# One-hot tiles of the expert gates: four single-token comparisons on VectorE replaced by one wide comparison there and a multiplication on GpSimd

## The chip, the cores and the metric

The kernel runs on one core of a Trainium2 chip. The metric is the device time of one execution in microseconds (us). Engines are named TensorE (PE in the profile), VectorE (DVE), ScalarE (ACT) and GpSimd (POOL). All data is 32-bit floating point.

## The reference

The reference is a chain of two small networks on 256 tokens with 1024 features. The last stage of each of the second network's two layers is a mixture over 16384 single-neuron experts. For each token, 8 heads choose 16 experts each, so 128 slots per token. An expert's number is a pair (i1, i2) of numbers below 128, and each slot has a weight `gate`:

```python
expert = i1 * PEER_NKEYS + i2
gate = jax.nn.softmax(score, axis=-1)
h = jnp.einsum('thkd,td->thk', u_tab[expert], zb)
act = gate * jax.nn.gelu(h, approximate=False)
return jnp.einsum('thk,thkd->td', act, v_tab[expert])
```

The kernel doesn't gather experts. It computes all 16384 for all tokens and multiplies by a dense table of gates, G[t, i1, i2], which is the sum of the weights of the token's slots that chose (i1, i2). For one token this table is a product of two matrices with the 128 slots as the summed dimension: A[slot, i1] = gate x (i1 is the slot's first number), B[slot, i2] = (i2 is the slot's second number). Both are one-hot in each row. The stage `PeerGates` builds A and B and multiplies them.

## The kernel before

The program is a list of stages. Each has a part for each engine, and the engines meet between stages at one counter, `stage_done`. Weights stream all the time through a ring of four blocks. Each block is split for the products into a rounded part (ScalarE, `round`) and the rest (GpSimd, `leave_rest`, L253, a tensor_tensor of 128x1024 that subtracts the one from the other). In the stage `Modulation`, at the program's start, VectorE takes over half of these subtractions, so that both engines run L253.

In a layer, `PeerRoute` finds the chosen experts with VectorE and GpSimd. Two of its lines return below. L2297 is a VectorE comparison (is_equal) of 128x512 elements, of a rank broadcast along the last dimension against the first 16 columns of the table of numbers. L2236 is GpSimd's multiplication of the resulting 128x256 elements in place by a broadcast row. L2241 adds halves on GpSimd. `PeerRoute` ends with a transpose that leaves `slot`, of shape [128 slots, 3, 256 tokens]: first number, second number, weight.

`PeerGates` then goes through the tokens in 128 sets of two (`SET = 2`), with four buffers (`BUFS = 4`) for the one-hot tiles `hot` of shape [128, buffer, A or B, token, 128]. For each token VectorE compares the constant row `iota` (0 to 127) with the token's column of `slot`: at L2356 against the first number, multiplying by the weight in the same instruction, and at L2357 against the second number. TensorE waits for `hot_ready` and issues one matmul per token (L2370) into PSUM; each appears as two records in the profile. ScalarE copies the 128x256 results of a set into the table of gates (L2386). VectorE waits for TensorE's `done` of the set that used its buffer before; TensorE waits for ScalarE's `kept`. GpSimd has no part in this stage. VectorE's part is written out without a loop; TensorE and ScalarE loop.

The stage `PeerExperts` follows, with products of 128x256 (L237 to L239) and the two VectorE instructions L2522 and L2525 per block. Its first instruction on VectorE is a memset, at L2515, which waits for the end of the gate stage.

Of the kernel before, what the change touches and what calls it, by code (L numbers as in the profile page):

```python
# [2 lines left out]

# [8 lines left out]
ALU = mybir.AluOpType  # L12
AX = mybir.AxisListType

P = 128
# [57 lines left out]
class Signals:  # L73


    def __init__(self, nc, ctx):
        self.nc, self.ctx, self.sems, self.total = nc, ctx, {}, {}
# [94 lines left out]
class Stage:  # L172
# [83 lines left out]
    def pe(self, pe):  # L256
        pass
# [4 lines left out]
    def dve(self, dve, link):  # L262
        pass

    def pool(self, pool, link):
        rounds = self.split // RING
        if rounds > 1:
            with pool.Fori(0, rounds) as it:
                for r in range(RING):
                    for h in range(2):  # L270
                        self.leave_rest(r, h, self.split_count(it * RING + r))
        else:
            rounds = 0
        for j in range(rounds * RING, self.split):
            for h in range(2):
                self.leave_rest(j, h, self.split_count(j))
# [49 lines left out]
class Modulation(Stage):  # L326
# [68 lines left out]
    def dve(self, dve, link):  # L395
        c, nc = self.chip, self.nc
        dve.wait_ge(self.chip.stage_done, self.index)
        dve.wait_ge(self.cond_rounded.sem, self.cond_rounded.at(1))
        nc.vector.tensor_tensor(self.parts[:, :, 2:4], self.cond, self.parts[:, :, 0:2].bitcast(F32), ALU.subtract)\
            .then_inc(self.cond_split.sem, 1)  # L400
        with dve.Fori(0, self.blocks // RING) as it:
            for r in range(RING):
                self.leave_rest(r, 1, self.split_count(it * RING + r), nc.vector)
        dve.wait_ge(self.turned.sem, self.turned.at(1))
        m = c.mods[:].rearrange("p j d s -> p (j d) s")
        b = columns(c.vec, "b_mod", self.layer, 72).unsqueeze(2).broadcast_to([P, 72, 2])
        turned = c.ps[:, 7, 0:288].rearrange("p (m s) -> p m s", s=4)
        link(nc.vector.tensor_tensor(m, turned[:, :, 0:2], b, ALU.add))
        link(nc.vector.tensor_tensor(m, m, turned[:, :, 2:4], ALU.add))
        for n in range(3):  # L410
            g = columns(c.vec, "norm_g", 3 * self.layer + n, KD).unsqueeze(2).broadcast_to([P, KD, 2])
            scale, gate = c.mods[:, 3 * n + 1, :, :], c.mods[:, 3 * n + 2, :, :]
            link(nc.vector.tensor_scalar(scale, scale, 1.0, None, ALU.add))
            link(nc.vector.tensor_tensor(scale, scale, g, ALU.mult))
            if n != 1:
                link(nc.vector.tensor_scalar(gate, gate, 0.5, None, ALU.mult))
        if self.start:
            dve.wait_ge(c.inputs_loaded, 16 * N_INPUTS)
            dve.wait_ge(self.start.stored.sem, self.start.stored.at(16))
        dve.sem_inc(c.stage_done, 1)  # L420


class Norm(Stage):
# [48 lines left out]
    def pe(self, pe):  # L472
# [6 lines left out]
        if self.keep:  # L479
# [3 lines left out]
            last.then_inc(self.x_kept.sem, 1)  # L483

    def dve(self, dve, link):
        c, nc = self.chip, self.nc
        dve.wait_ge(self.chip.stage_done, self.index)
# [1840 lines left out]
class PeerGates(Stage):  # L2328
# [9 lines left out]
    def __init__(self, chip):  # L2338
        super().__init__(chip)
        self.slot = chip.at(G_SLOT, 3, N)  # L2340
        self.hot = chip.at(G_HOT, self.BUFS, 2, self.SET, P)
        self.gates = chip.at(G_GATES, N * NKEYS)
        self.hot_ready = chip.signals("hot_ready", self.SETS)
        self.done = chip.signals("gates_done", self.SETS)
        self.kept = chip.signals("gates_kept", self.SETS)

    def dve(self, dve, link):
        v, iota = self.nc.vector, self.chip.iota
        dve.wait_ge(self.chip.stage_done, self.index)
        for n in range(self.SETS):  # L2350
            r = n % self.BUFS
            if n >= self.BUFS:
                dve.wait_ge(self.done.sem, self.done.at(n - self.BUFS + 1))
            for i in range(self.SET):
                first, second, gate = [self.slot[:, a, n * self.SET + i:n * self.SET + i + 1] for a in range(3)]
                v.tensor_scalar(self.hot[:, r, 0, i], iota, first, gate, ALU.is_equal, ALU.mult)  # L2356
                last = v.tensor_scalar(self.hot[:, r, 1, i], iota, second, None, ALU.is_equal)  # L2357
            last.then_inc(self.hot_ready.sem, 1)

    def pe(self, pe):  # L2360
        pe.wait_ge(self.chip.stage_done, self.index)

        def body(it, first=False):
            for r in range(self.BUFS):
                n = it * self.BUFS + r
                pe.wait_ge(self.hot_ready.sem, self.hot_ready.at(n + 1))
                if not first:
                    pe.wait_ge(self.kept.sem, self.kept.at(n - self.BUFS + 1))
                for i in range(self.SET):
                    last = self.nc.tensor.matmul(self.chip.ps[:, r, i * P:(i + 1) * P], self.hot[:, r, 0, i], self.hot[:, r, 1, i],  # L2370
                                                 start=True, stop=True)
                last.then_inc(self.done.sem, 1)

        body(0, first=True)
        with pe.Fori(1, self.SETS // self.BUFS) as it:
            body(it)
# [481 lines left out]
```

## Time and profile before

| | |
|---|---|
| median of three runs | 5390.88 us (5387.66 to 5395.12) |
| profiled execution, its own time | 5387.66 us |
| its span, first to last instruction | 5385.6 us |
| busy: TensorE, GpSimd, VectorE, ScalarE | 4776, 2937, 2793, 1934 us |
| the two gate stages | 117.3 and 117.4 us |

Busy shares are averages over stages with different limits. A group's busy time counts each instant once, and its mean is that of one instruction from start to end; where instructions of an engine overlap, the mean is longer than the distance from start to start.

### The profile page before, as it was taken

The numbers are of one execution on the slowest core, as the hardware profiler recorded it, in microseconds if no ns is written. First come the engines' busy times: TensorE is split into PE (matmuls) and PEld (weight loads), VectorE is DVE, ScalarE is ACT, GpSimd is POOL, SyncE is SP. The second block draws the span as 40 slices with busy tenths as digits, with TensorE's granted clock in tenths as the row PEclk, the third lists the DMA queues.
The fourth block names the chain that finished last, engine by engine and source line by source line (L and its number), as shares of the span: only waits on it lengthen the run. The fifth ranks groups of instructions, "written<-read, shape, count | busy, mean of one in ns | idle before, by whom it ended". The sixth has DMA issues, their size and how long they took to land.

```text
span 5385.6 us, 77857 instructions
## 1 busy us (share of the span) xinstructions
PE 4776.2 (89%) x30280; PEld 4183.4 (78%) x30280; DVE 2793.4 (52%) x4012; ACT 1934.3 (36%) x2791; POOL 2937.4 (55%) x1298
## 2 busy tenths in 40 slices
PE   6899899969999989898874899999898865999998
PEld 2587777727778879787873899999877864899998
DVE  6410221182110431345569777777444669777776
ACT  5322332262223234332232444444431233444443
POOL 6444144484434358651262588887640351688886
PEclk9999999999999999987787999999986888999999
DMA  8322122272223234440030344445430120344443
GB/s 311 117 94 89 53 78 94 100 267 86 94 79 109 86 118 173 151 164 1 24 126 0 114 174 177 173 176 181 154 133 1 48 102 0 134 178 172 178 173 139
DMA packets 92447, 649.46 MB, mean 121 GB/s; under 512 B 9824, under 2 KB 14048, under 8 KB 14432
## 3 DMA queue, kind: packets, MB, share of 16 engines
q1 hardware_dynamic: 87120, 634.25, 32.9%
q10 hardware_dynamic: 5136, 12.49, 0.6%
q8 instruction: 141, 2.31, 0.2%
q14 instruction: 50, 0.41, 0.0%
HBM read 642.50 MB, written 4.19 MB: 120 GB/s over the span
## 4 chain that ended last, share of the span: by engine, by line
PE 59%; DVE 21%; DMA 8%; issue 5%; POOL 4%; ACT 3%; ACTq 0%; SPq 0%; POOLq 0%; DVEq 0%
PE ps L237 16%; PE ps L238 16%; PE ps L239 16%; DMA ring<-in_weights 8%; DVE part L2525 5%; POOL ring_rest L253 4%; DVE arena L2356 2%; DVE arena L2357 2%; PE ps L1334 1%; PE ps L477 1%; DVE arena L506 1%; PE ps L1302 1%; ACT part L2477 1%; DVE arena L1963 1%; ACT rounded L224 1%
## 5 line engine op out<-in xcount | busy, mean ns | idle before, releaser
L253 POOL TENSOR_TENSOR ring_rest<-ring,rounded 128x1024 fp32r<-128x1024 f32 x1104 | 2776.0, 2537 | 1893.1 <-ACT rounded L224 1365.7
L237 PE MATMUL ps<-part,rounded 128*128 128x256 f32 (+1 forms) x5760 | 1853.4, 322 | 151.5 <-DVE part L499 64.7
L238 PE MATMUL ps<-part,rounded 128*128 128x256 f32 (+1 forms) x5760 | 1835.5, 319 | 0.0
L239 PE MATMUL ps<-part,ring_rest 128*128 128x256 f32 (+1 forms) x5760 | 1827.0, 317 | 0.0
L237 PEld LDWEIGHTS ps<-part,rounded 128*128 128x128 f32 x5760 | 1101.5, 191 | 285.9 <-issue 67.7
L238 PEld LDWEIGHTS ps<-part,rounded 128*128 128x128 f32 x5760 | 1101.2, 191 | 77.4
L239 PEld LDWEIGHTS ps<-part,ring_rest 128*128 128x128 f32 x5760 | 1095.1, 190 | 70.9
L224 ACT ACTIVATE rounded<-ring 128x1024 fp32r<-128x1024 f32 x672 | 671.1, 1050 | 800.6 <-PE ps L239 713.2
L2525 DVE TENSOR_TENSOR part<-arena,part 128x256 fp32r<-128x256 f32 x256 | 605.7, 2366 | 211.3 <-ACT part L2477 211.3
L2492 ACT ACTIVATE rounded<-ring 128x1024 fp32r<-128x1024 f32 x504 | 531.7, 1055 | 410.0 <-DMA ring<-in_weights 408.1
L237 PE MATMUL ps<-x_parts,rounded 128*128 128x256 f32 x2304 | 652.3, 283 | 12.2 <-DVE x_parts L499 11.0
L238 PE MATMUL ps<-x_parts,rounded 128*128 128x256 f32 x2304 | 653.8, 284 | 0.0
L239 PE MATMUL ps<-x_parts,ring_rest 128*128 128x256 f32 x2304 | 649.5, 282 | 0.0
L2522 DVE TENSOR_TENSOR arena<-arena 128x256 f32<-128x256 f32 x256 | 530.4, 2072 | 183.9 <-ACT arena L2471 183.6
L237 PEld LDWEIGHTS ps<-x_parts,rounded 128*128 128x128 f32 x2304 | 439.9, 191 | 14.3 <-issue 12.6
L238 PEld LDWEIGHTS ps<-x_parts,rounded 128*128 128x128 f32 x2304 | 437.8, 190 | 0.0
L239 PEld LDWEIGHTS ps<-x_parts,ring_rest 128*128 128x128 f32 x2304 | 434.5, 189 | 0.0
L586 DVE TENSOR_TENSOR part<-ps,arena 128x512 f32<-128x512 f32 (+1 forms) x88 | 55.0, 625 | 525.2 <-ACT arena L575 525.2
L648 DVE SCALAR_TENSOR_TENSOR x<-ps,mods,x 128x256 f32<-128x256 f32 x80 | 31.9, 475 | 522.1 <-PE ps L239 522.1
L575 ACT ACTIVATE arena<-ps 128x512 f32<-128x512 f32 (+1 forms) x88 | 47.9, 544 | 572.8 <-PE ps L239 572.7
L2471 ACT ACTIVATE arena<-ps 128x256 f32<-128x256 f32 x256 | 98.5, 385 | 406.6 <-PE ps L239 377.8
L253 DVE TENSOR_TENSOR ring_rest<-ring,rounded 128x1024 fp32r<-128x1024 f32 x72 | 228.0, 3193 | 6.7 <-ACT rounded L224 6.7
(324 smaller groups left out, 4805.4 us busy)
## 6 DMA issues: line engine op xcount, KB each, us to landing
ring<-in_weights SPq DMA_DIRECT2D x600, 1024.0 KB, 4.8
arena<-bias_scratch ACTq DMA_DIRECT2D x2, 2048.0 KB, 8.7
bias_scratch<-arena ACTq DMA_DIRECT2D x1, 3072.0 KB, 8.7
x<-in_x SPq DMA_DIRECT2D x1, 2048.0 KB, 20.7
arena<-in_keys ACTq DMA_DIRECT2D x2, 1024.0 KB, 4.9
arena<-in_bias_in SPq DMA_DIRECT2D x1, 1216.0 KB, 8.5
arena<-in_cst SPq DMA_DIRECT2D x1, 1216.0 KB, 21.8
arena<-in_expo ACTq DMA_DIRECT2D x1, 1024.0 KB, 5.4
```

What stands on the lines that cost most here:

```text
L224: self.nc.scalar.activation(c.rounded[:, s % ROUNDED, half], c.ring[:, slot, half], ACT.Copy)\
L237: mm(out, w[0], a[0], start=start, stop=False)
L238: mm(out, w[0], a[1], start=False, stop=False)
L239: return mm(out, w[1], a[0], start=False, stop=stop)
L253: eng.tensor_tensor(c.ring_rest[:, slot, half], c.ring[:, slot, half], c.rounded[:, (self.s0 + r) % ROUNDED, half].bitcast(F32), ALU.subtr ...
L586: v.tensor_tensor(self.h[:, j, :], self.chip.ps[:, 2 * (j % 2) + 1, 0:self.t], self.silu[:, j % 2, :], ALU.mult)\
L2356: v.tensor_scalar(self.hot[:, r, 0, i], iota, first, gate, ALU.is_equal, ALU.mult)
L2357: last = v.tensor_scalar(self.hot[:, r, 1, i], iota, second, None, ALU.is_equal)
L2471: copy(self.gelu[:, r % 2, :], c.ps[:, r % 2, 0:N], ACT.Gelu).then_inc(self.gelu_ready.sem, 1)
L2492: self.nc.scalar.activation(c.rounded[:, (self.s0 + r) % ROUNDED, half], c.ring[:, f % RING, half], ACT.Copy)\
L2522: v.tensor_tensor(gelu, gelu, self.gates[:, :, bass.ds(b, 1)].rearrange("p t a -> p (t a)"), ALU.mult)\
L2525: v.tensor_tensor(self.parts[1][:, r % 2, :], gelu, self.parts[0].bitcast(F32)[:, r % 2, :], ALU.subtract)\
```

## The change

VectorE's part becomes a loop with one instruction per set: it compares `iota`, broadcast over A and B and over the two tokens, with the first and second numbers of both tokens, and writes all four one-hot tiles, 128x512 elements. The weight is no longer multiplied in there. GpSimd gets a part in the stage: for each set it waits for `hot_ready` and multiplies the two A tiles (128x256 elements) in place by the tokens' weights, broadcast along the tile. TensorE waits for GpSimd's signal `weighted` instead of `hot_ready`. The rest of TensorE's part and ScalarE's are unchanged. (Blank lines added at the top of the file shift its line numbers.)

```diff
+        self.weighted = chip.signals("weighted", self.SETS)
 ...
     def dve(self, dve, link):
-        v, iota = self.nc.vector, self.chip.iota
         dve.wait_ge(self.chip.stage_done, self.index)
-        for n in range(self.SETS):
-            r = n % self.BUFS
-            if n >= self.BUFS:
-                dve.wait_ge(self.done.sem, self.done.at(n - self.BUFS + 1))
-            for i in range(self.SET):
-                first, second, gate = [self.slot[:, a, n * self.SET + i:n * self.SET + i + 1] for a in range(3)]
-                v.tensor_scalar(self.hot[:, r, 0, i], iota, first, gate, ALU.is_equal, ALU.mult)
-                last = v.tensor_scalar(self.hot[:, r, 1, i], iota, second, None, ALU.is_equal)
-            last.then_inc(self.hot_ready.sem, 1)
+        wide = [P, 2, self.SET, P]
 
         def body(it, first=False):
             for r in range(self.BUFS):
                 n = it * self.BUFS + r
+                if not first:
+                    dve.wait_ge(self.done.sem, self.done.at(n - self.BUFS + 1))
+                self.nc.vector.tensor_tensor(self.hot[:, r], self.chip.iota.unsqueeze(1).unsqueeze(1).broadcast_to(wide),
+                                             self.slot[:, 0:2, bass.ds(n * self.SET, self.SET)].unsqueeze(3).broadcast_to(wide),
+                                             ALU.is_equal).then_inc(self.hot_ready.sem, 1)
+
+        body(0, first=True)
+        with dve.Fori(1, self.SETS // self.BUFS) as it:
+            body(it)
+
+    def pool(self, pool, link):
+        pool.wait_ge(self.chip.stage_done, self.index)
+        with pool.Fori(0, self.SETS // self.BUFS) as it:
+            for r in range(self.BUFS):
+                n = it * self.BUFS + r
+                hot = self.hot[:, r, 0]
+                pool.wait_ge(self.hot_ready.sem, self.hot_ready.at(n + 1))
+                self.nc.gpsimd.tensor_tensor(hot, hot, self.slot[:, 2, bass.ds(n * self.SET, self.SET)].unsqueeze(2)
+                                             .broadcast_to([P, self.SET, P]), ALU.mult).then_inc(self.weighted.sem, 1)
 ...
-                pe.wait_ge(self.hot_ready.sem, self.hot_ready.at(n + 1))
+                pe.wait_ge(self.weighted.sem, self.weighted.at(n + 1))
```

## Rows read from the trace of the kernel before

**Rows 1.** The page: its span, and the chain's shares by line.
```profile
span 5385.6 us, 77857 instructions
...
PE ps L237 16%; PE ps L238 16%; PE ps L239 16%; DMA ring<-in_weights 8%; DVE part L2525 5%; POOL ring_rest L253 4%; DVE arena L2356 2%; DVE arena L2357 2%; PE ps L1334 1%; PE ps L477 1%; DVE arena L506 1%; PE ps L1302 1%; ACT part L2477 1%; DVE arena L1963 1%; ACT rounded L224 1%
```

**Rows 2.** Windows, the gate stage of each layer: length, busy us, clock, DMA.
```profile
2880.20:2997.50 117.30, 91.41 (x512) 68.22 (x512) 115.90 (x512) 49.19 (x128) 0.00 (x0) 0.98 0.00 0
4477.80:4595.20 117.40, 91.24 (x512) 68.21 (x512) 115.95 (x512) 49.26 (x128) 0.00 (x0) 0.98 0.00 0
```

**Rows 3.** Groups in layer 0's gate stage: busy, mean ns, idle before.
```profile
L2370 PE MATMUL ps<-arena 128*128 128x128 f32 x512 | 91.4, 304 | 25.8 <-DVE arena L2357 22.0
L2356 DVE TENSOR_SCALAR arena<-cst,arena 128x128 f32<-128x128 f32 x256 | 89.8, 351 | 5.8 <-ACTq L2226 5.8
L2357 DVE TENSOR_SCALAR arena<-cst,arena 128x128 f32<-128x128 f32 x256 | 74.3, 290 | 0.0
```

**Rows 4.** Waits in layer 0's gate stage: us in total, times, longest.
```profile
ACT arena L2386 <- PE ps L2370: 67.5, 126, 2.5
...
PE ps L2370 <- DVE arena L2357: 22.0, 93, 1.6
```

**Rows 5.** Timeline of VectorE: start, duration; before and in the stage.
```profile
2849.98 0.69 DVE L2297 TENSOR_TENSOR arena<-arena,cst 128x512 f32<-128x512 f32 x1
...
2850.59 0.69 DVE L2297 TENSOR_TENSOR arena<-arena,cst 128x512 f32<-128x512 f32 x1
...
2880.24 0.35 DVE L2356 TENSOR_SCALAR arena<-cst,arena 128x128 f32<-128x128 f32 x1 [5.79 <-ACTq L2226]
...
2995.84 0.29 DVE L2357 TENSOR_SCALAR arena<-cst,arena 128x128 f32<-128x128 f32 x1
2997.55 0.17 DVE L2515 MEMSET arena<- 128x128 f32 x1 [1.41 <-ACTq L2389]
```

**Rows 6.** Timeline of TensorE in the gate stage.
```profile
2881.38 4.34 PE L2370 MATMUL ps<-arena 128*128 128x128 f32 x20 [1.64 <-DVE arena L2357]
...
2930.22 1.54 PE L2370 MATMUL ps<-arena 128*128 128x128 f32 x8 [0.20 <-DVE arena L2357]
```

**Rows 7.** Three lines in the whole run: duration ns min/median/max, starts, forms.
```profile
L2297 DVE TENSOR_TENSOR arena<-arena,cst x32: 682/691/2827, 2794.7 to 4466.6; 128x512 f32<-128x512 f32 x32
...
L2236 POOL TENSOR_TENSOR arena<-arena x64: 718/724/903, 2800.7 to 4471.7; 128x256 f32<-128x256 f32 x64
...
L253 POOL TENSOR_TENSOR ring_rest<-ring,rounded x1104: 2337/2412/4437, 33.3 to 5357.7; 128x1024 fp32r<-128x1024 f32 x184
L253 DVE TENSOR_TENSOR ring_rest<-ring,rounded x72: 1210/3340/3389, 38.1 to 1181.4; 128x1024 fp32r<-128x1024 f32 x72
```

**Rows 8.** Timeline of GpSimd and VectorE in layer 0's routing stage.
```profile
2851.36 2.77 POOL L2236 TENSOR_TENSOR arena<-arena 128x256 f32<-128x256 f32 x4 [3.11 <-DVE arena L2297]
...
2868.44 0.69 DVE L2297 TENSOR_TENSOR arena<-arena,cst 128x512 f32<-128x512 f32 x1
...
2868.51 2.83 POOL L253 TENSOR_TENSOR ring_rest<-ring,rounded 128x1024 fp32r<-128x1024 f32 x1
...
2869.05 2.83 DVE L2297 TENSOR_TENSOR arena<-arena,cst 128x512 f32<-128x512 f32 x1
```

**Rows 9.** Timeline of VectorE in the modulation stage, first and last of six.
```profile
53.03 3.34 DVE L253 TENSOR_TENSOR ring_rest<-ring,rounded 128x1024 fp32r<-128x1024 f32 x1
...
69.59 3.33 DVE L253 TENSOR_TENSOR ring_rest<-ring,rounded 128x1024 fp32r<-128x1024 f32 x1
```

**Rows 10.** GpSimd's groups by shape in the whole run.
```profile
L2241 POOL TENSOR_TENSOR arena<-arena 128x512 f32<-128x512 f32 x16 | 20.1, 1259 | 1.3
...
L2241 POOL TENSOR_TENSOR arena<-arena 128x256 f32<-128x256 f32 x16 | 11.5, 721 | 1.3
```

**Rows 11.** Windows: the modulation stage, and the gate stage's start.
```profile
0.00:141.00 141.00, 93.08 (x336) 32.03 (x336) 99.64 (x33) 82.60 (x100) 98.67 (x36) 1.00 0.84 311
...
2880.20:2883.00 2.80, 1.62 (x7) 1.65 (x8) 2.76 (x13) 0.30 (x1) 0.00 (x0) 0.50 0.00 0
```

More of the change, by code:

```diff
@@ L2347, in dve, with body @@
     def dve(self, dve, link):
-        v, iota = self.nc.vector, self.chip.iota
         dve.wait_ge(self.chip.stage_done, self.index)
-        for n in range(self.SETS):
-            r = n % self.BUFS
-            if n >= self.BUFS:
-                dve.wait_ge(self.done.sem, self.done.at(n - self.BUFS + 1))
-            for i in range(self.SET):
-                first, second, gate = [self.slot[:, a, n * self.SET + i:n * self.SET + i + 1] for a in range(3)]
-                v.tensor_scalar(self.hot[:, r, 0, i], iota, first, gate, ALU.is_equal, ALU.mult)
-                last = v.tensor_scalar(self.hot[:, r, 1, i], iota, second, None, ALU.is_equal)
-            last.then_inc(self.hot_ready.sem, 1)
+        wide = [P, 2, self.SET, P]
+        def body(it, first=False):
+            for r in range(self.BUFS):
[11 more added lines that the diff above has]
+        with pool.Fori(0, self.SETS // self.BUFS) as it:
+            for r in range(self.BUFS):
+                n = it * self.BUFS + r
+                hot = self.hot[:, r, 0]
+                pool.wait_ge(self.hot_ready.sem, self.hot_ready.at(n + 1))
+                self.nc.gpsimd.tensor_tensor(hot, hot, self.slot[:, 2, bass.ds(n * self.SET, self.SET)].unsqueeze(2)
+                                             .broadcast_to([P, self.SET, P]), ALU.mult).then_inc(self.weighted.sem, 1)
     def pe(self, pe):
```

## The prediction

> **What bounds the kernel now.** I read the page first, for the chain that ended last. It runs mostly through TensorE's three products per weight tile, but two lines of the gate stage, L2356 and L2357, hold 2% each of 5385.6 us [rows 1]. That is about as much as the two runs of this stage last, so wherever the stage is busy on VectorE, the chain goes through it.
>
> Next I cut the trace to the stage, once for each layer. It lasts 117.3 and 117.4 us; VectorE is busy for 115.9 of them, TensorE for 91, ScalarE for 49, GpSimd for nothing, and no transfer runs [rows 2]. VectorE is therefore the only candidate for the bound. The groups of instructions inside the stage say the same: 512 VectorE instructions of 128x128, mean 0.35 and 0.29 us, with no idle before them but the 5.8 us in which the stage is opened [rows 3]. In the waits, ScalarE waits for TensorE 126 times and TensorE for VectorE [rows 4]. The reader should see a pipeline with one full engine and three that follow it.
>
> The means overlap (each starts before the one ahead has ended), so the pace must come from start times, not from busy sums. VectorE's first starts at 2880.24 and its last ends at 2995.84 + 0.29 = 2996.13 [rows 5]: 115.9 us for 128 sets of two tokens, or **0.905 us a set**. The first instruction of the next stage comes at 2997.55, 1.4 us after VectorE's last; the tail (matmuls, the ScalarE copy, the stage signal) is that long.
>
> How much faster could the others go? TensorE issues two sets (8 records) in 1.54 us when both are ready, 0.77 us a set; at the stage's start it needs 4.34 us for five sets, 0.87 each [rows 6].
>
> **The change, part by part.** Per set it removes four VectorE instructions of 128x128 and adds one VectorE tensor_tensor of 128x512 (both comparisons of both tokens) and one GpSimd tensor_tensor of 128x256 (the weight, in place). TensorE now waits for the weighted tile. The buffers (four), the 128 sets, matmuls and copies stay.
>
> *VectorE alone.* The trace has the very form: L2297, an is_equal of 128x512 f32 from the same table of numbers against a broadcast operand, takes 0.682 us at least, median 0.691 [rows 7]. Two follow each other at 2849.98 and 2850.59 [rows 5], a pace of 0.61 us. Against 0.905 that is a gain of 0.30 us a set, 75 us in 256 sets, if VectorE were all that mattered.
>
> *GpSimd alone.* L2236 is also the very form (128x256, multiply, broadcast operand, in place): 0.718 us at least [rows 7]. Four in a row last 2.77 us [rows 8], so their pace is (2.77 - 0.72) / 3 = 0.68. A set would then be ready every 0.68 to 0.72 us, if GpSimd were undisturbed.
>
> *Both together.* This is the step on which everything hangs. When a tensor_tensor of one of the two engines runs while the other has one too, the second one stops. At 2868.51 GpSimd starts one that lasts 2.83 us instead of 2.34 (its start falls in VectorE's 0.69 us), and VectorE's next L2297, begun at 2869.05, takes 2.83 us instead of 0.69; it ends at 2871.88, about 0.54 us after GpSimd's end at 2871.34 [rows 7, 8]. So they take turns. The new stage consists of nothing but such pairs: both new instructions read two operands from SBUF, and each set needs one of each.
>
> What does a pair cost when they take turns all the time? The modulation stage shows it, with 1024 elements on each: VectorE's starts go from 53.03 to 69.59 in five steps, 3.31 us a pair, while alone they need 1.210 and 2.337, together 3.55 [rows 7, 9]. So 0.24 us of the two durations overlaps: the fixed part of one is spent while the other holds the way. To scale to our sizes I take off what fewer elements save: on VectorE 1.210 - 0.682 = 0.528 us (1024 to 512), on GpSimd 2.337 - 0.718 = 1.619 us (1024 to 256). 3.31 - 0.53 - 1.62 = **1.16 us a set**. A second reading: from the end of VectorE's first L2297 (2869.13) to the end of its second (2871.88) are 2.75 us with one GpSimd instruction of 1024 between; less 1.62 that is 1.13 [rows 8]. I take 1.16, since it comes from a long steady stretch.
>
> The Trainium skill, page "SBUF — State Buffer", section "Who interferes with whom", has it as an exclusive lock, held for the full instruction, between a VectorE instruction with two SBUF inputs and a GpSimd one that reads SBUF. The turns in the trace agree with it [rows 8], but the full length doesn't: durations laid end to end would be 3.55 us in the modulation stage, where 3.31 is measured. By the page's full length this change would cost about 127 us, by the row about 66.
>
> *The sum.* (1.16 - 0.905) x 256 = 65.3, with the unrounded 1.165 66.6 us. Filling the pipeline: before, the first matmul came 1.14 us after VectorE's first start [rows 5, 6]; now 0.69 + 0.72 and two signals, about 1.65, so +0.5 us in each layer, +1. The tail is the same. GpSimd's new work lies ahead of its first subtraction for the experts, but that one waits for a ScalarE rounding that comes after the stage anyway, and GpSimd was idle in the stage [rows 2]; nothing is late there but by what the stage itself is late. VectorE's queue has nothing else in the stage either. The waits with a computed address in the loop cost some tens of ns each; they fall in the time in which the other engine has its turn: nothing. Four buffers suffice: a set goes from VectorE to the end of its matmuls in about 0.7 + 1.2 + 0.9 us, and four sets last 4.6.
>
> Total +67.6 us on this execution's 5387.66: 5455.3. The median shown is 3.2 us higher, which gives **5458 us**.
>
> *Bounds of the pair.* Below: only the time per element, no fixed part at all. VectorE's 512 elements are 0.53 us by the difference above; GpSimd's 256 are 1259 - 721 = 0.54 us [rows 10]. 1.07 us a set, +42 us in all: 5434. Above, with the turns kept but no overlap of fixed parts: the paces alone, 0.61 + 0.68 = 1.29 us, +98: 5490.
>
> **The rivals.**
> *Full durations in turn.* If each hands over only after its whole duration, and signals fall between, a set costs 0.69 + 0.72 = 1.41 us: +129, 5520. The 3.31 us of the modulation stage speak against it; for it, that here each is started by a signal of another engine rather than always standing ready. This is what the page's rule above would give.
> *No turns (the other side).* If the two new instructions don't hinder each other, say because one operand is a broadcast column, the bound is TensorE at 0.77 us a set (GpSimd at 0.68 is just below). (0.77 - 0.905) x 256 = -35 us, +1 for filling: 5357. It decides from a pair below 0.905 us. Against it: L2297 has a broadcast operand too and was stopped [rows 8].
> *Turns without overlap,* 1.29 us: 5490, as above. It would come from irregular turns, two of one engine and then two of the other, since VectorE can run up to four sets ahead.
> *TensorE's clock.* It is at 0.50, so at 1.2 GHz, over the stage's first 2.8 us after an idle stretch [rows 11]. TensorE would now be busy for about 0.71 of 1.16 us, 61% instead of 78%. In the modulation stage it is busy for 66% and the granted clock is 1.00 [rows 11], so I expect 2.4 GHz to stay. If not, even 0.87 us a set stays hidden below 1.16, and only the first microseconds of the experts would run slower, some 2 us a layer.
>
> **How the numbers follow.** Turns with overlap, 1.07 to 1.22 us a set (5434 to 5472): 0.65. Turns without overlap, up to 1.33: 0.15. Full durations: 0.10. No turns: 0.08. Something that cancels out near zero: 0.02. A measurement of this kernel tells a change from none from about 0.2%, 11 us. The range takes the first two cases with a margin at its ends, 5430 to 5500, and leaves out 0.2. Slower by over 0.2%: 0.90; within: 0.02; faster: 0.08.
>
> **What the profile after would show.** The stage should last about 150 us in each layer. VectorE's new instruction should have a mean well over 0.69 us (near 1.2, as it starts, waits its turn, and ends), GpSimd's over 0.72, and the two busy sums together should exceed the stage's length, with neither engine idle for long. TensorE should wait for GpSimd in each set. Everything outside the two stages should keep its length. The prediction is wrong in its mechanism if VectorE's instruction stays at 0.69 while GpSimd is busy, and wrong in size if the starts of successive sets lie elsewhere than 1.1 to 1.2 us apart.

## The result and the profile after

The changed kernel takes 5428.12 us (median of four runs, 5416.47 to 5430.32; three more took 5424.21 to 5431.33) against 5389.78 us before: a ratio of 1.0067 with a 95% interval of 1.0053 to 1.0082. Later five more runs gave 5420.73 us and 1.0063 (1.0049 to 1.0077). It is slower by 0.6 to 0.7%, some 30 to 38 us. 5458 us was forecast, with 5430 as the low end: the sign was right, and the size was almost twice too large.

The windows of the two gate stages answer to [rows 2]. The columns are length, busy time of TensorE, its weight loads, VectorE, ScalarE and GpSimd, then granted clock and transfers.

```profile
2878.50:3010.70 132.20, 92.42 (x513) 69.30 (x513) 129.66 (x128) 49.07 (x129) 129.80 (x128) 0.97 0.00 0
4489.90:4622.00 132.10, 92.36 (x513) 69.33 (x513) 129.57 (x129) 49.03 (x128) 129.82 (x128) 0.97 0.00 0
```

Each stage lasts 132.1 us and not 117.3, so 14.8 us more, 29.6 for both. The two profiled executions differ by 5416.47 - 5387.66 = 28.8 us, so between these two the stages hold the whole difference. VectorE and GpSimd are both busy for 130 of 132 us, although 128 instructions at 0.61 us each, the pace that the prediction had for VectorE alone, would fill only 78.

The instructions of the two new lines (duration ns min/median/max), which answer to [rows 7], and the waits of layer 0's stage, which answer to [rows 4]:

```profile
L2370 DVE TENSOR_TENSOR arena<-cst,arena x256: 682/1095/1100, 2878.6 to 4618.3; 128x512 f32<-128x512 f32 x128
```

```profile
L2385 POOL TENSOR_TENSOR arena<-arena x256: 606/1056/1059, 2879.5 to 4619.9; 128x256 f32<-128x256 f32 x128
```

```profile
ACT arena L2414 <- PE ps L2398: 82.9, 127, 3.3
PEld ps L2398 <- issue: 49.9, 92, 2.8
PE ps L2398 <- POOL arena L2385: 39.5, 120, 2.4
```

The shortest of each line, 0.682 and 0.606 us, is what it needs alone; the median is 0.41 and 0.45 us longer. TensorE's matmuls now wait for GpSimd, 120 times, and its weight loads 30 times more. The timeline shows the order (start, duration). On VectorE, the first and the seventh of seven in a row; on GpSimd, the one that belongs between the first two:

```profile
2899.16 1.09 DVE L2370 TENSOR_TENSOR arena<-cst,arena 128x512 f32<-128x512 f32 x1
...
2905.27 1.10 DVE L2370 TENSOR_TENSOR arena<-cst,arena 128x512 f32<-128x512 f32 x1
```

```profile
2899.67 1.06 POOL L2385 TENSOR_TENSOR arena<-arena 128x256 f32<-128x256 f32 x1
```

Six steps in 6.11 us are **1.018 us a set**. VectorE's instruction ends at 2900.25, GpSimd's at 2900.73, VectorE's next at 2901.27: each ends about half a microsecond after the other's end, 0.48 us for GpSimd's turn and 0.54 for VectorE's. They alternate without a gap through the whole stage: between one start of GpSimd's and its next there is exactly one of VectorE's, in 126 of 127 cases.

The first instruction of the next stage starts 2.45 us after VectorE's last has ended, where it was 1.41 before [rows 5]:

```profile
3010.70 0.17 DVE L2543 MEMSET arena<- 128x128 f32 x1 [2.45 <-ACTq L2417]
```

### The profile page after: what moved, and what is told of

Read it like the earlier page. It is cut to its first block, busy times and chain, and to the rows that moved or that the text cites. A ratio compares the mean times of both kernels' runs of the same rounds, so it can differ in the third digit from the quotient of the medians.

```text
span 5414.7 us, 78578 instructions
## 1 busy us (share of the span) xinstructions
PE 4785.0 (88%) x30280; PEld 4187.1 (77%) x30280; DVE 2834.1 (52%) x3244; ACT 1929.9 (36%) x2791; POOL 3203.7 (59%) x1554
## 4 chain that ended last, share of the span: by engine, by line
PE 57%; DVE 17%; DMA 8%; POOL 8%; issue 6%; ACT 3%; POOLq 0%; ACTq 0%; SPq 0%; DVEq 0%
PE ps L250 16%; PE ps L251 16%; PE ps L252 16%; DMA ring<-in_weights 8%; DVE part L2553 5%; POOL ring_rest L266 4%; POOL arena L2385 3%; PE ps L1347 1%; PE ps L490 1%; DVE arena L519 1%; ACT part L2505 1%; DVE arena L1976 1%; ACT rounded L237 1%; PE ps L1663 1%; PE ps L1315 1%
## 5 line engine op out<-in xcount | busy, mean ns | idle before, releaser
L2553 DVE TENSOR_TENSOR part<-arena,part 128x256 fp32r<-128x256 f32 x256 | 610.1, 2383 | 207.6 <-ACT part L2505 207.6
L2370 DVE TENSOR_TENSOR arena<-cst,arena 128x512 f32<-128x512 f32 x256 | 259.3, 1088 | 11.6 <-ACTq L2239 11.6
L2385 POOL TENSOR_TENSOR arena<-arena 128x256 f32<-128x256 f32 x256 | 259.6, 1051 | 6.0 <-DVE arena L2370 6.0
L2398 PE MATMUL ps<-arena 128*128 128x128 f32 x1024 | 184.7, 307 | 79.3 <-POOL arena L2385 79.2
```

The lines of the kernel that those rows point to most:

```text
L2370: self.nc.vector.tensor_tensor(self.hot[:, r], self.chip.iota.unsqueeze(1).unsqueeze(1).broadcast_to(wide), self.slot[:, 0:2, bass.ds(n * ...
L2385: self.nc.gpsimd.tensor_tensor(hot, hot, self.slot[:, 2, bass.ds(n * self.SET, self.SET)].unsqueeze(2) .broadcast_to([P, self.SET, P]), AL ...
L2553: v.tensor_tensor(self.parts[1][:, r % 2, :], gelu, self.parts[0].bitcast(F32)[:, r % 2, :], ALU.subtract)\
```

## The experiments

In all of them the length given is that of layer 0's stage, unless said otherwise, taken from VectorE's first instruction to the memset that opens the next stage, so that work outside, which wanders by up to 14 us between executions, stays out of it.

### The changed kernel again (again)

No edit; another execution is profiled, since the spread between executions (5416 to 5431) asked for one.

> The changed kernel once more, nothing edited. Its profiled execution took 5416.5 us, the other six 5424 to 5431. Theory 1 (the gate stages set the difference between executions, as the order of turns varies): a profile of another execution shows a set every 1.018 us in one stage and something else, near 1.1 us, in the other or in both. Theory 2 (the difference lies outside): both gate stages last 132.1 us again and the ratio stays near 1.007.

5420.73 us (5419.55 to 5430.22), and its profiled execution took 5426.93, 10.5 more than the first. The stage runs from 2892.3 to 3024.4, 132.1 us, as before. Theory 2 holds: the stage repeats to 0.1 us, and the spread lies outside, where the same stage begins at 2878.6 in one profile and at 2892.3 in the other.

### VectorE's constant read from PSUM (psum)

```diff
     def dve(self, dve, link):
         dve.wait_ge(self.chip.stage_done, self.index)
+        dve.wait_ge(self.iota_kept.sem, self.iota_kept.at(1))
 ...
-                self.nc.vector.tensor_tensor(self.hot[:, r], self.chip.iota.unsqueeze(1)...
+                self.nc.vector.tensor_tensor(self.hot[:, r], self.chip.ps[:, 3, 0:P].unsqueeze(1)...
 ...
     def act(self, act, link):
+        self.nc.scalar.activation(self.chip.ps[:, 3, 0:P], self.chip.iota, ACT.Copy).then_inc(self.iota_kept.sem, 1)
 ...  (matmuls and copies: bank r % 2 in place of r, TensorE waits for the copy of set n - 2)
```

> The table 0 to 127 is read by VectorE from PSUM (copied there by ScalarE at the stage's start), so that VectorE's comparison has only one operand in SBUF; the matmuls use two banks of PSUM in turn, not four. All else as changed. Theory A (the two engines take turns for a way into SBUF that VectorE's second SBUF operand needs): they now run side by side, VectorE's instruction takes about 0.65 to 0.75 us, GpSimd's 0.61, and the stage goes by TensorE's 0.77 us a set or by the slowest of the three: about 100 to 105 us, total some 30 us below the kernel before (5360). Theory B (they hinder each other whatever VectorE reads, for instance since both write SBUF): a set every 1.02 us as in the changed kernel, total near 5425.

5335.46 us against 5390.19, ratio 0.9906 (0.989 to 0.9922). The stage takes 87.7 us in layer 0 and 86.5 in layer 1, less than the 100 to 105 that I expected, since I had put TensorE at 0.77 us a set. Its two lines, and the window of the first stage:

```profile
L2372 DVE TENSOR_TENSOR arena<-ps,arena x256: 678/690/693, 2884.5 to 4537.9; 128x512 f32<-128x512 f32 x128
```

```profile
L2387 POOL TENSOR_TENSOR arena<-arena x256: 612/612/614, 2885.4 to 4538.8; 128x256 f32<-128x256 f32 x128
```

```profile
2884.10:2972.20 88.10, 81.48 (x513) 68.83 (x513) 82.34 (x128) 49.30 (x129) 77.45 (x128) 0.95 0.00 0
```

The same two instructions, on the same number of elements, no longer stretch each other: 0.69 and 0.61 us at the median. Both still write SBUF, so theory B falls. What made them take turns is VectorE's second operand in SBUF. In layer 0 the stage gains 44.4 us on the changed kernel and 29.6 on the kernel before. The Trainium skill, page "SBUF — State Buffer", section "Who interferes with whom", says that a VectorE instruction with at most one SBUF input outside its two-port modes doesn't contend with GpSimd; the 0.69 and 0.61 us agree.

### The banks alone (banks_only)

The changed kernel with the bank edit of psum and nothing else.

> The changed kernel with the matmuls writing two banks of PSUM in turn, not four, and nothing else: the side effect that the psum variant had. If the gain of psum came from VectorE's operand in PSUM alone, a set every 1.02 us and stages of 132 us, as changed. If the banks had a part in it, the stage is shorter than 132 us.

5410.99 us in one run. The stage lasts 132.2 us, from 2879.5, and the two lines have medians of 1.096 and 1.057 us. The banks had no part in the gain. (That the run lies below the changed kernel's 5416 to 5431 comes from outside the stages, which last as long as there.)

### GpSimd's operand in the form of the row that I used (rows16)

```diff
-                ...tensor_tensor(hot, hot, self.slot[:, 2, bass.ds(n * self.SET, self.SET)].unsqueeze(2)
-                                             .broadcast_to([P, self.SET, P]), ALU.mult)
+                short = hot.rearrange("p i (k j) -> p (i k) j", j=TOPK)
+                ...tensor_tensor(short, short, self.slot[:, 2, 0:TOPK].unsqueeze(1)
+                                             .broadcast_to([P, self.SET * P // TOPK, TOPK]), ALU.mult)
```

> GpSimd's multiplication takes the form of the row that the prediction used (rows of 16 elements times one row of 16 weights, broadcast over the rows), for the same 128x256 elements; it leaves out the right weights, so the result differs. Theory A (the form of the second operand sets GpSimd's time: 0.718 us for this form against 0.606 alone for a broadcast column): a set every 1.13 to 1.16 us, the stage about 146 to 149 us, the total near 5450. Theory B (GpSimd's time depends on the number of elements alone, and 1.018 us comes from a better overlap of fixed parts): a set every 1.02 us, the stage 132 us.

The kernel leaves out the right weights: it multiplies as many elements, but by others. 5453.87 us in one run; the stage lasts 146.7 us. GpSimd's line, and VectorE's first and sixth of six in a row:

```profile
L2386 POOL TENSOR_TENSOR arena<-arena x256: 718/1170/1177, 2889.8 to 4657.9; 128x256 f32<-128x256 f32 x128
```

```profile
2938.93 1.21 DVE L2370 TENSOR_TENSOR arena<-cst,arena 128x512 f32<-128x512 f32 x1
...
2944.60 1.21 DVE L2370 TENSOR_TENSOR arena<-cst,arena 128x512 f32<-128x512 f32 x1
```

Five steps in 5.67 us are 1.134 us a set. GpSimd's shortest is 0.718 us, that of L2236 in [rows 7], and 0.112 us over the changed kernel's; the set is 0.116 us longer. With this operand the forecast of the stage would have been nearly right (1.16 and 1.13 had been worked out). Theory A holds.

### Twice the work on GpSimd (weigh_all)

```diff
-                ...tensor_tensor(hot, hot, self.slot[:, 2, bass.ds(n * self.SET, self.SET)].unsqueeze(2)
-                                             .broadcast_to([P, self.SET, P]), ALU.mult)
+                ...tensor_tensor(self.hot[:, r], self.hot[:, r], self.slot[:, 1:3, bass.ds(n * self.SET, self.SET)].unsqueeze(3)
+                                             .broadcast_to([P, 2, self.SET, P]), ALU.mult)
```

> GpSimd multiplies all four tiles of a set (128x512 elements, broadcast columns) in place of the two A tiles; B is thereby multiplied too, so the result differs. Theory A (turns: a set costs VectorE's turn of 0.54 us plus GpSimd's): GpSimd's turn grows by its time for 256 elements, 0.43 us, a set every 1.45 us, the stage about 186 us. Theory B (no turns, the slowest engine sets the pace): GpSimd alone at about 1.04 us, the stage about 135 us.

GpSimd multiplies all four tiles, 128x512 elements, so B too, which the right result doesn't have. 5540.6 us in one run; the stage lasts 187.6 us. GpSimd's line, and the window of the stage:

```profile
L2385 POOL TENSOR_TENSOR arena<-arena x256: 1039/1487/1490, 2883.8 to 4740.2; 128x512 f32<-128x512 f32 x128
```

```profile
2882.90:3070.50 187.60, 155.75 (x513) 118.83 (x513) 183.77 (x129) 49.16 (x128) 184.78 (x128) 0.50 0.00 0
```

VectorE's starts go from 2939.12 to 2943.46 in three steps, 1.447 us a set: 0.43 more than in the changed kernel, as GpSimd's shortest is 0.433 longer. Turns, as theory A had it; without them GpSimd alone would have set 1.04.

Three sizes now give one rule for this pair. The pace is the sum of what the two need alone, less 0.27 us: 0.682 + 0.606 - 1.018 = 0.270, with rows16 0.684 + 0.718 - 1.134 = 0.268, with weigh_all 0.682 + 1.039 - 1.447 = 0.274. (What each needs alone is taken from the shortest in its line, for VectorE one of a stage's first two instructions, for GpSimd a stage's last, which have no partner.)

### No weights, and no GpSimd (no_weight)

GpSimd's part and its signal are taken out, and the kernel leaves out the weights; TensorE waits for `hot_ready`.

> GpSimd's multiplication is left out (the weights are missing from the result); TensorE waits for VectorE's comparison. It shows what the wide comparison is worth without a partner. Turns theory: VectorE's instruction takes 0.69 us at a pace of 0.61, and TensorE sets the pace at 0.68 us a set (as with the operand in PSUM), stage about 88 us. Rival: VectorE's instruction stays near 1.09 us with GpSimd idle, and then its length had nothing to do with GpSimd.

5312.01 us in one run. VectorE's instruction takes 0.685 us at the median and the stage 79.2 us, from 2884.2 to 2963.4. Its length was GpSimd's doing, and the rival falls. The pace is 0.61 us a set, VectorE's own; my 0.68 for TensorE was wrong, and so was the prediction's 0.77, as it kept up with 0.61.

### Both on VectorE (all_vector)

```diff
+        def weigh(n, r):
+            hot = self.hot[:, r, 0]
+            dve.wait_ge(self.hot_ready.sem, self.hot_ready.at(n + 1))
+            self.nc.vector.tensor_tensor(hot, hot, self.slot[:, 2, ...]..., ALU.mult).then_inc(self.weighted.sem, 1)
 ...
                 self.nc.vector.tensor_tensor(self.hot[:, r], ..., ALU.is_equal).then_inc(self.hot_ready.sem, 1)
+                if not (first and r == 0):
+                    weigh(n - 1, (r - 1) % self.BUFS)
 ...  (GpSimd's part is taken out)
```

> Both new instructions on VectorE, GpSimd idle, the multiplication of a set issued behind the comparison of the next. Turns theory: VectorE pays 0.61 us for the comparison and some 0.34 for 256 elements of multiplication, 0.95 us a set, stage about 123 us: about 20 us faster in all than the changed kernel, and about 11 us slower than the kernel before (5401). Rival: the split over two engines buys something in spite of the turns, and this version is slower than 1.02 us a set.

5399.75 us (ten runs) against 5391.17, ratio 1.0011 (1.0001 to 1.0021). The stage lasts 121.7 us. VectorE's timeline:

```profile
2940.17 0.68 DVE L2376 TENSOR_TENSOR arena<-cst,arena 128x512 f32<-128x512 f32 x1
2940.77 0.42 DVE L2368 TENSOR_TENSOR arena<-arena 128x256 f32<-128x256 f32 x1
2941.11 0.68 DVE L2376 TENSOR_TENSOR arena<-cst,arena 128x512 f32<-128x512 f32 x1
```

0.60 + 0.34 = 0.94 us a set. The split over two engines is worse than no split, by 10.4 us a layer. The reason stands in the numbers: while they take turns, a multiplication costs the pair GpSimd's 0.48 us, and VectorE does it in 0.34; the comparison is only 0.06 us dearer there (0.60 and not 0.54).

### Two buffers (bufs2)

`BUFS = 2` in the changed kernel.

> The changed kernel with two buffers in place of four. The prediction held that four suffice, since a set goes from VectorE to the end of its matmuls in some 2.8 us. Then four buffers are well above what turns need, and two are not: a buffer's way is about 0.7 + 0.6 + 0.8 us and three signals, 2.3 us, so a set every 1.15 to 1.2 us, stage about 150 us. If a set still comes every 1.02 us, the depth of buffers plays no part at all; if the two engines then mostly don't overlap, VectorE's instruction gets short (0.69 us) as well.

5620.18 us in one run; the stage lasts 227.2 us, 1.77 us a set, far over my 1.15 to 1.2. Its window:

```profile
2892.10:3119.30 227.20, 132.38 (x512) 113.86 (x512) 88.52 (x128) 49.28 (x128) 109.41 (x128) 0.50 0.00 0
```

VectorE's instruction is short (0.693 us median), but it waited for TensorE 126 times, 135.4 us in all. TensorE's granted clock is 0.50, so 1.2 GHz, in the whole stage, and its records last 421 ns and not 275. That four buffers carry the turns without a gap is shown (both engines busy for 130 of 132 us). With two, a set's way from VectorE's start to TensorE's signal takes 3.40 us, and VectorE starts 0.13 us after that: 3.53 us for two sets, 1.77 each. Of the 3.40, TensorE's part, from GpSimd's end on, takes 1.53 us, in the changed kernel 0.87. How much of these 0.66 us is the slower clock and how much the copies (`BUFS` also sets the number of PSUM banks, and TensorE's weight loads waited 63 times for ScalarE) was not parted. By an estimate, with 0.87 a set would still take 1.44 us, so more than half of the loss is the shorter chain.

### The same remedy in the expert stage (psum_gelu, gelu_only)

Both have one edited line, the first on top of psum, the second on the kernel before:

```diff
-        self.gelu = chip.at(G_GELU, 2, N)
+        self.gelu = chip.ps[:, 2:4, 0:N]
```

> The psum variant, and besides the experts' activation held in PSUM (banks 2 and 3) in place of SBUF, so that the two VectorE instructions of each expert block have one operand in SBUF each. Now they take 2.1 and 2.4 us, of which most is GpSimd's turn. If turns are the cause there too, they take about 0.4 us, and the block falls from 6.0 us to TensorE's 5.8 or so: another 30 to 50 us off psum's time, about 5295. If TensorE and the weight stream already set the pace of the blocks, the instructions get short and the total stays at psum's 5335.

> The kernel before with the experts' activation in PSUM alone, the gate stage untouched. It parts psum_gelu's gain in two. Turns in the expert stage: VectorE's two instructions there fall from 2.1 and 2.4 us to about 0.6 and 0.4, the expert stages get shorter by what psum_gelu had over psum, some 92 us: 5299 in all, gate stages 117.3 us as before. If the two changes helped each other, it would be less.

psum_gelu takes 5243.46 us, ratio 0.9719 (0.9696 to 0.9742): 92 us less than psum, where 30 to 50 were expected. gelu_only takes 5311.52, ratio 0.9858 (0.9827 to 0.989), so 78 us less than the kernel before, where I expected 91; its four runs lie from 5296 to 5329. VectorE's two instructions of the expert stage in the kernel before, and then in psum_gelu:

```profile
L2522 DVE TENSOR_TENSOR arena<-arena x256: 625/2121/2810, 3002.4 to 5359.9; 128x256 f32<-128x256 f32 x128
...
L2525 DVE TENSOR_TENSOR part<-arena,part x256: 424/2425/2454, 3003.7 to 5361.1; 128x256 fp32r<-128x256 f32 x128
```

```profile
L2553 DVE TENSOR_TENSOR ps<-ps,arena x256: 609/628/639, 2980.2 to 5216.0; 128x256 f32<-128x256 f32 x128
...
L2556 DVE TENSOR_TENSOR part<-ps,part x256: 424/425/427, 2981.5 to 5217.1; 128x256 fp32r<-128x256 f32 x128
```

The medians fall from 2.1 and 2.4 us to 0.63 and 0.43. The turns with GpSimd are gone there too, and the windows of 500 us in the middle of the expert stage show what TensorE does with that, first in the kernel before, then in psum_gelu:

```profile
3100.00:3600.00 500.00, 493.02 (x4007) 480.71 (x4006) 378.36 (x167) 226.80 (x334) 413.50 (x168) 1.00 0.49 176
```

```profile
3100.00:3600.00 500.00, 500.00 (x4248) 500.00 (x4247) 93.19 (x177) 233.39 (x353) 422.72 (x178) 1.00 0.52 186
```

It was busy for 98.6% already, but in the same time 4248 of its records pass and not 4007, 6% more. The busy share of matmuls hid room that the count shows. The starts of L2553 are 5.65 us apart and those of L2522 5.99, and I had put TensorE's limit at 5.8: 0.33 us in each of 256 blocks are some 85 of the 92 us. gelu_only's profiled execution, 5300.92 us, has the same 4248 records in this window and gate stages of 117.3 and 117.4 us, so there the two edits neither help nor hinder each other. Why two of its runs lie some 25 us higher no profile shows.

### Three banks (three_banks)

psum_gelu with the results of successive sets in banks 0, 1, 2, 1; TensorE waits for the copy before last in odd sets only.

> The psum_gelu kernel with the matmuls of successive sets in banks 0, 1, 2, 1 and not 0, 1, 0, 1. There a set took 0.675 us, though VectorE's comparison manages 0.61 alone and TensorE kept up with it (no_weight, four banks). If the hand-over of two banks between TensorE and ScalarE makes the difference, a set comes every 0.61 to 0.64 us, and each stage is 4 to 8 us shorter: about 5233 in all. If it is GpSimd's or VectorE's own pace, the stage stays at 88 us.

5247.34 us, ratio 0.973 (0.9714 to 0.9746), no faster than psum_gelu, and a stage of 86.8 us against 87.8 in layer 0, 86.4 against 86.5 in layer 1. The hand-over of banks makes at most 1 us of the 9 that part psum's stage from no_weight's.

What else keeps a set at about 0.65 us, when comparison and multiplication take 0.61 each, can be read from psum's trace: the way round the four buffers. From VectorE's start on a set to TensorE's `done` for it are 2.45 us on average (the moment of the signal is that at which ScalarE, which waits for it too, goes on). The comparison that uses the buffer again starts 0.16 us later on average, so 2.61 us for four sets, 0.65 each. In the changed kernel VectorE starts 0.61 us after that signal, and in no_weight 0.84 us, so there the signal is early. This is read, not tested: no run has more than four buffers.

## Why the size was wrong, step by step

**What bounds the stage before: right.** VectorE set 0.905 us a set, and with the instructions changed the stages grew by 29.6 us, where the two profiled executions differ by 28.8.

**VectorE alone: right.** 0.682 us at least was read from L2297, and 0.682 was measured; the pace of 0.61 appears in no_weight.

**GpSimd alone: the step that failed.** The prediction said that "L2236 is also the very form" and took 0.718 us from it. The new multiplication takes 0.606 us at its shortest. It isn't the same form: L2236 multiplies rows of 16 elements by one row of 16, the change multiplies runs of 128 by one number each. A nearer row was in the trace and I passed over it, the multiplication of the attention stage (L1479), in place by a column that is broadcast along the run. Its groups in the kernel before (busy us, mean ns, idle before):

```profile
L1479 POOL TENSOR_TENSOR arena<-arena 128x1024 f32<-128x1024 f32 x12 | 22.7, 1894 | 62.0 <-DVE arena L1463 57.6 <-DVE arena L1458 4.4
...
L1479 POOL TENSOR_TENSOR arena<-arena 128x512 f32<-128x512 f32 x12 | 12.5, 1041 | 40.8 <-DVE arena L1463 35.4 <-DVE arena L1458 5.5
```

(1894 - 1041) / 512 is 1.67 ns an element, and 1041 - 256 x 1.67 = 614 ns for 256 elements. That would have given 1.16 - 0.10 = 1.06 us a set. rows16 is the proof: with the operand of L2236 the set goes back to 1.134.

**Both together: right in kind, 0.03 us off.** They take turns, each new instruction lengthened by its wait for the other, as the prediction described it. It took 0.24 us of overlap from the modulation stage; 0.27 was measured at three sizes. The miss of 1.165 - 1.018 = 0.147 us a set is thus 0.112 of GpSimd's own time and 0.03 of overlap. The stage's starts were thus 1.018 us apart, where the prediction named 1.1 to 1.2, and the stage lasts 132 us, not 150.

**The bounds: too high.** The lower one, 1.07 us, was meant to hold no fixed part at all and still lies over the 1.018 measured, since its 0.54 us for GpSimd's 256 elements came from L2241, whose operands are of yet another form (2.1 ns an element, where L1479 has 1.67). In weigh_all 256 elements more cost 0.433 us, which would have made the bound 0.96. A bound from a row of another form is no bound.

**The tail: wrong, and small.** The prediction said "The tail is the same" and put +0.5 us a layer at the filling. But VectorE doesn't wait for the first matmul, so a later one (2880.50 - 2878.59 = 1.9 us after VectorE's first start, 1.65 was forecast) lengthens nothing by itself. The longer way of a set shows at the end, where GpSimd's multiplication follows VectorE's last comparison: 2.45 us and not 1.41, +1.0 a layer. VectorE's own stretch grew from 115.9 to 129.7 us, 13.8, and the two together are the 14.8 that each stage shows.

**Buffers and queues: right.** The profiled runs differ by 28.8 us and the stages by 29.6, so nothing of note was added elsewhere.

**The rivals.** Full durations in turn (1.41 us) is excluded by 1.018: even the shorter 0.682 + 0.606, laid end to end, would be 1.29 us. The Trainium skill, page "SBUF — State Buffer", section "Terms", has the shared ports "held for the full instruction"; the turns agree with it, the full length as the profile counts it doesn't, by 0.27 us. Turns without overlap (1.29 us) was to come from an irregular order, and the order was regular. No turns (0.77 us) is excluded in the changed kernel. psum shows that the choice of an operand can end the turns, though not in the way that this rival named (a broadcast column): it took an operand outside SBUF, and then the change pays some 30 us a layer. The 0.77 us for TensorE was itself too long, since it kept up with 0.61 in no_weight. TensorE's clock: 0.97 in the stage, as I expected.

**What stays open.** The medians differ by 30 to 38 us and the stages by 29.6. The rest, up to some 8 us, lies outside the stages, where single profiles wander by as much; whether it is chance wasn't settled. Why 0.27 us of the two durations overlap, and why GpSimd's time depends on the operand's pattern, isn't shown by any run.

## What to carry to other kernels

Before moving work from VectorE to an idle GpSimd, ask whether the two will take turns: here, with both running tensor_tensor on operands in SBUF, a set cost the sum of both less 0.27 us, and the split was dearer than leaving the work on VectorE. With one of VectorE's operands in PSUM, each instruction took what it needs alone; on this kernel that turned +0.7% into -0.9%, and the same remedy at a second place, one edited line, visible as VectorE instructions of three to six times their shortest duration, brought the total to -2.8%. When a duration is borrowed from a row, match the pattern of the operands and not only the shape and the operation.

## What was unexpected in the hardware

GpSimd's time for a multiplication of 128x256 elements depends on the operand's pattern: 0.606 us with a number broadcast along runs of 128 (the changed kernel), 0.718 with rows of 16 (rows16, and L2236 in the kernel before).

TensorE's clock stayed at the low level in stages in which it was busy for much of the time. In weigh_all it was granted 0.50, so 1.2 GHz, over the whole stage with a busy share of 155.75 / 187.6 = 83% (a share that the low clock itself lengthens), in bufs2 0.50 with 58%; in the changed kernel it began at 0.50 after the same idle stretch and rose to 1.00, 2.4 GHz. The windows of the changed kernel's stage show the rise:

```profile
2878.50:2883.00 4.50, 2.50 (x10) 2.42 (x11) 4.41 (x6) 0.61 (x3) 3.52 (x4) 0.50 0.00 0
2883.00:2888.00 5.00, 4.90 (x24) 4.27 (x22) 5.00 (x6) 2.08 (x6) 5.00 (x6) 0.61 0.00 0
2888.00:3008.00 120.00, 83.24 (x472) 61.21 (x471) 120.00 (x119) 45.19 (x118) 120.00 (x119) 1.00 0.00 0
```

With a set every 1.02 us the clock rose after some 8 us, with one every 1.45 us it never did. In rows16, with one every 1.13 us, it did both: in layer 0 it was 0.50 for the first 11 us, then went up and down (0.75 on average over the next 68 us) and was 1.00 from there on; in layer 1 it rose once, after some 12 us, and stayed. In weigh_all the low clock cost nothing in the pace, which the turns set.
